# Two-block transformer kernel: the delta rule's decay steps a step later, the forgetting attention from long to short units, the last attention's scores in three pieces

## What is computed

```python
# forgetting attention: 16 heads of 64, query blocks of 128, causal
for i in range(S // BLK):
    lo, hi = i * BLK, (i + 1) * BLK
    s = einsum('bhqd,bhkd->bhqk', q[:, :, lo:hi], k[:, :, :hi]) * scale
    s = s + F[:, :, lo:hi, None] - F[:, :, None, :hi]
    p = softmax(where(causal, s, -inf), axis=-1)
    outs.append(einsum('bhqk,bhkd->bhqd', p, v[:, :, :hi]))

# delta rule, chunks of 128, 8 heads, once forward and once backward
decay = exp(where(tril, gc[..., :, None] - gc[..., None, :], -inf))
m = where(strict, einsum('bhncd,bhnsd->bhncs', kb, kc) * decay, 0.0)
tmat = triangular_solve(m + eye, eye, ...)          # the inverse
qk = einsum('bhncd,bhnsd->bhncs', qc, kc) * decay
def step(s, inp):
    v_new = u_i - w_i @ s
    o_i = qd_i @ s + qk_i @ v_new
    s = s * gl_i + kd_i.T @ v_new

# grouped-query attention: 8 heads of 64 on 2 key heads, 768 keys for each of 512 queries
o = softmax(q @ k.T * scale) @ v
```

## Time and profile before

| what | us |
| --- | --- |
| median of 3 runs (lowest, highest) | 3141.66 (3140.93, 3143.12) |
| the profiled execution | 3141.73 |
| its span in the profile | 3139.9 |
| PE busy in the span (22796 matmuls) | 2968.0 (95%) |
| DVE, ACT, POOL busy | 1669.5 (53%), 1214.1 (39%), 309.4 (10%) |
| forgetting attention, first score to last output | 661.04 to 758.18 |
| delta rule, steps 0 to 10 | 1337.03 to 1582.59 |
| GQA | about 2562 to 2638 |

### The profile page before, as it was taken

The page is one execution under the profiler, slowest core; times in us unless marked ns, Lnnn a source line. Parts: engine busy times, 40 slices in busy tenths (PEclk is TensorE's granted clock), DMA queues, the critical chain, the costliest instruction groups (busy, mean ns, idle before and its releaser), DMA issues.

```text
span 3139.9 us, 53876 instructions
## 1 busy us (share of the span) xinstructions
PE 2968.0 (95%) x22796; PEld 2420.2 (77%) x22796; DVE 1669.5 (53%) x2942; ACT 1214.1 (39%) x2193; POOL 309.4 (10%) x449
## 2 busy tenths in 40 slices
PE   7999999999999999978889999999999999999998
PEld 4767787766777688778766788888888877788887
DVE  3245666455533656677755553555556636554444
ACT  4315435356441455433345552111114437642221
POOL 1010020000001000043330010111110101000000
PEclk9999999989999999988889999999999999999999
DMA  6285542210314722001020022333342341032321
GB/s 230 81 296 183 187 156 89 94 55 18 106 69 173 264 101 71 22 18 29 24 69 28 1 74 81 124 120 119 121 146 76 93 75 48 8 107 101 107 94 67
DMA packets 180585, 308.11 MB, mean 98 GB/s; under 512 B 24038, under 2 KB 58151, under 8 KB 180089
## 3 DMA queue, kind: packets, MB, share of 16 engines
q1 hardware_dynamic: 141408, 253.87, 24.2%
q0 software_dynamic: 12048, 40.24, 4.2%
q10 hardware_dynamic: 26889, 10.56, 1.2%
HBM read 296.47 MB, written 6.81 MB: 97 GB/s over the span
## 4 chain that ended last, share of the span: by engine, by line
PE 78%; DVE 12%; ACT 6%; DMA 2%; issue 1%; POOL 0%; ACTq 0%; DVEq 0%; POOLq 0%
PE psum L428 20%; PE psum L429 20%; PE psum L430 20%; PE psum L1229 2%; DVE weights_r L370 2%; PE psum L2723 2%; PE psum L1257 1%; PE psum L1245 1%; DMA weights<-in_w_mod 1%; PE psum L621 1%; PE psum L2713 1%; DVE arena L917 1%; PE psum L1006 1%; PE psum L2825 1%; PE psum L1040 1%
## 5 line engine op out<-in xcount | busy, mean ns | idle before, releaser
L370 DVE TENSOR_TENSOR weights_r<-weights,weights_r 128x2048 fp32r<-128x2048 f32 (+1 forms) x161 | 360.5, 2259 | 379.9 <-ACT weights_r L361 379.9
L361 ACT ACTIVATE weights_r<-weights 128x2048 fp32r<-128x2048 f32 (+1 forms) x161 | 302.4, 1896 | 649.2 <-DMA weights<-in_w_ffn_gate 218.9
L428 PE MATMUL psum<-feat_r,weights_r 128*128 128x512 f32 (+1 forms) x1536 | 540.0, 352 | 1.2 <-ACT arena L2498 1.0
L429 PE MATMUL psum<-feat_r,weights_r 128*128 128x512 f32 (+1 forms) x1536 | 537.5, 350 | 0.0
L430 PE MATMUL psum<-feat_r,weights_r 128*128 128x512 f32 (+1 forms) x1536 | 536.7, 349 | 0.0
L428 PE MATMUL psum<-weights_r,feat_r 128*128 128x512 f32 (+2 forms) x1344 | 522.4, 389 | 12.1 <-DVE feat_r L762 8.8
L430 PE MATMUL psum<-weights_r,feat_r 128*128 128x512 f32 (+2 forms) x1344 | 517.4, 385 | 0.0
L429 PE MATMUL psum<-weights_r,feat_r 128*128 128x512 f32 (+2 forms) x1344 | 516.9, 385 | 0.0
L428 PEld LDWEIGHTS psum<-feat_r,weights_r 128*128 128x128 f32 x1536 | 294.4, 192 | 44.4 <-issue 5.4
L430 PEld LDWEIGHTS psum<-feat_r,weights_r 128*128 128x128 f32 x1536 | 293.9, 191 | 37.1
L429 PEld LDWEIGHTS psum<-feat_r,weights_r 128*128 128x128 f32 x1536 | 294.4, 192 | 36.3
(11 more groups left out here) (534 smaller groups left out, 4284.0 us busy)
## 6 DMA issues: line engine op xcount, KB each, us to landing
weights<-in_w_mod SPq DMA_DIRECT2D x30, 2048.0 KB, 16.6
weights<-in_gla_w_in SPq DMA_DIRECT2D x24, 1024.0 KB, 7.4
arena<-in_w_mod_turned POOLq DMA_DIRECT2D x96, 256.0 KB, 3.2
weights<-in_w_ffn_gate SPq DMA_DIRECT2D x22, 1024.0 KB, 6.9
weights<-in_w_ffn_up SPq DMA_DIRECT2D x22, 1024.0 KB, 5.1
weights<-in_w_ffn_down SPq DMA_DIRECT2D x20, 1024.0 KB, 6.9
weights<-in_fox_w_in SPq DMA_DIRECT2D x16, 1024.0 KB, 6.7
weights<-in_sgu_w_in SPq DMA_DIRECT2D x12, 1024.0 KB, 6.6
```

Source lines behind the costliest of these rows:

```text
L361: act.e.activation(WEI_r[:, s * SLOT + HALF:s * SLOT + HALF + n], WEI_t[:, s * SLOT:s * SLOT + n], ACT.Copy).then_inc(*A.put(("weights", c ...
L370: dve.e.tensor_tensor(WEI_r[:, s * SLOT:s * SLOT + n], WEI_t[:, s * SLOT:s * SLOT + n], WEI_r[:, s * SLOT + HALF:s * SLOT + HALF + n].bitc ...
L428: pe.e.matmul(ps, lh, rh, start=first, stop=False)
L429: pe.e.matmul(ps, lh, rl, start=False, stop=False)
```

## The change

Four edits. No instruction is added or taken away on DVE and POOL; ACT gets one more (the table load that stood ahead of the first exponential now belongs to it), and PE two more matmuls for each of GQA's 16 pairs.

- Delta rule, DVE: `dve_dif` and `dve_clamp` leave the end of step n-1 (where they worked for n+1) and stand in step n: the difference behind `dve_e(n,0)`, the clamp behind `dve_state(n)`. `dve_g(n,0)` stands ahead of `dve_state(n)`, and `dve_e(n,1)` ahead of `dve_kk(n+1)`.
- Delta rule, ACT: `act_decay_relu(n+1)` moves behind `act_cross(n-1)`, `act_decay_exp(n+1)` behind `act_et(n,1)`.
- Forgetting attention: the units run from t = 3 to t = 0, and ACT issues an exponential of one column (`act_exp_table`) ahead of its wait, so that the table is loaded there.
- GQA: the scores of a head are cut into three pieces of 256 columns, and the six pieces of a pair alternate between the two heads; the wait on itself stands before the fifth.

```diff
@@ pe_wide
-            for n, j in ((0, 0), (1, 0), (1, 1), (0, 1)):
+            count = len(units[2 * p]["scores"])
+            for n, j in ((0, 0), (1, 0), (1, 1), (0, 1)) if count < 3 else [(n, j) for j in range(count) for n in range(2)]:
                 unit = units[2 * p + n]
-                if j < len(unit["scores"]):
+                if j < count:
                     lt, rh, n0, w, first, end = unit["scores"][j]
                     c0 = n * unit["nk"] + n0
-                    if (n, j) == (0, 1):
+                    if (n, j) == (0, count - 1) and count > 1:
                         pe.wait_ge(*B.of((tag, "middle", p)))
                     done = pe.e.matmul(ps[:, c0:c0 + w], lt, rh, start=first, stop=end)
-                    if (n, j) == (1, 0) and len(unit["scores"]) > 1:
+                    if (n, j) == (1, 0) and count > 1:
                         done.then_inc(*B.put((tag, "middle", p)))
-                    if (n, j) == (1, 1):
+                    if (n, j) == (1, 1) and count == 2 or (n, j) == (0, 2):
                         done.then_inc(*B.put())
@@ fox_units
-        for t in LAT:
+        for t in LAT[::-1]:
@@ act_fox
         A.mark((T, "in"))
+        act_exp_table(act)
         act.wait_ge(*V.of((T, "in")))
@@ act_gdn
             if behind:
                 act_join_v(act, n - 1)
-            if more:
-                act_decay_relu(act, n + 1)
-                act_decay_exp(act, n + 1)
-            if behind:
                 act_join_z(act, n - 1)
                 act_cross(act, n - 1)
                 act_rows(act, n + 2)
+            if more:
+                act_decay_relu(act, n + 1)
             act_et(act, n, 1)
+            if more:
+                act_decay_exp(act, n + 1)
             if behind:
                 act_corner(act, n - 1)
@@ dve_gdn
             dve_e(dve, n, 0)
+            if more and behind:
+                dve_dif(dve, n + 1)
+            dve_g(dve, n, 0)
             dve_state(dve, n)
-            dve_g(dve, n, 0)
+            if more and behind:
+                dve_clamp(dve, n + 1)
             dve_x(dve, n, 0)
+            dve_e(dve, n, 1)
             if more:
                 dve_kk(dve, n + 1, 0)
                 dve_kk(dve, n + 1, 1)
-            dve_e(dve, n, 1)
             dve_g(dve, n, 1)
...
             dve_vb(dve, n)
-            if n + 2 < STEPS:
-                dve_dif(dve, n + 2)
-                dve_clamp(dve, n + 2)
@@ gqa_units
-                                          for n0, w in WIDE_CUTS[hh % 2]],
+                                          for n0, w in ((0, 256), (256, 256), (512, 256))],
```

## The result

The changed kernel takes 3218.61 us (median of four, 3212.28 to 3226.34), the kernel before 3142.39 beside it: a ratio of 1.024 (95% interval 1.021 to 1.026). It is slower, as forecast, but by 76 us and not by 15; the time lies outside the range of 3135 to 3168. The profiled execution took 3219.32 us with a span of 3217.5, so 77.6 more than the span of before, 3139.9.

A forecast was written before the change was run, and what follows sets the result against it. PE, holding 78% of the chain, was taken as the bound, running back to back outside the attentions and delta rule. 3141.7 + 21 (delta rule) - 2 (forgetting attention) - 4 (GQA) gave 3156 us, range 3135 to 3168.

The forecast's parts named there:

- Where the time goes: Delta rule: the 1.8 us idle ahead of `pe_e2(n,0)` goes; about 2.6 us comes ahead of `pe_kq(n,1)`, awaiting `dve_kk`.
- (1): Delta rule: the clock stays up despite the 2.6 us idle; 3135 us in all; chance 0.10.
- (2): At `pe_kq(n,1)`: PE does not wait for `dve_kk`, DVE alone sets 19.1 us steps; 3111 us; chance 0.08.
- (3): Delta rule: exponential starts earlier, `dve_kk` comes 1 us sooner, +8 there, 3143 to 3144 us in all; chance 0.12.
- The step at full clock: Delta rule: a step takes 21.4 us against 19.7, +1.7 each, +18.7 over steps 0 to 10.
- The low time: Delta rule: low clock stays 6.8 us a step, only later in the step; step 2 newly gets it, costing 2.7.
- 0.40 us per us: Delta rule: each us of low clock lengthens a step by 0.40 us, taken from the old steps' lengths.
- The upper bound: Delta rule: at most +30 us around about +21, with 5 more if all low time lies on PE's path.
- Step 11 and what follows: Delta rule's last step: nothing of the changed order's cost runs there, so the sum counts steps 0 to 10 only.
- Forgetting attention: Table load hidden -1.3, shorter last value products -1.5, longer first pair 0.5 to 0.8; sum -2 us.
- the rival inside the term: Forgetting attention's end: low clock reaches 3.4 to 6.8 us into the z layer, giving +1.4; no chance given.
- GQA: Scores of a pair take about 1.6 us against 1.86, -4 us over 16 pairs; with per-matmul overhead, 2.4 gained.

The follow-up runs named there:

- `gdn_alone`: The kernel before with only the delta rule's new order on VectorE and ScalarE; 3219.92 us (ratio 1.024).
- filled kernel: The changed kernel plus three extra 64x512 matmuls behind each corner product, in PE's idle ahead of the query-key products; 3168.08 us (ratio 1.007).
- `before_filled`: The kernel before plus four extra 128x256 matmuls ahead of join v in each step, in place of the 1.81 us idle; 3154.08 us (ratio 1.003).
- kernel with one extra matmul: The changed kernel plus one extra 64x512 matmul behind each corner product; 3177.26, 3206.46, 3216.55 and 3221.07 us in four executions.
- `three_parts`: The kernel before with first turn ahead of difference and clamp, clamp ahead of state product, GQA's three pieces and the early table load; 3133.62 us (ratio 0.997).

## Why the prediction was wrong, point by point

**Where the time goes: right.** The idle ahead of `pe_e2(n,0)` goes, one ahead of `pe_kq(n,1)` comes, ended by L3049 in each of steps 1 to 10, and it costs. (Its evidence was thinner than it says: two of the four waits of the earlier trace rows are weight loads'.) `gdn_alone` carries the whole loss. Rivals (1), (2) and (3) are all out: the clock does not stay up, PE does wait for `dve_kk`, and the exponential does not come sooner.

**The step at full clock: right, to a tenth.** The filled kernel lets it be read in its step 8 (zero 1532.92), beside step 6 of the changed kernel (zero 1501.42):

| point of the step, us | predicted | filled, full clock | changed, mostly 1.2 GHz |
|---|---|---|---|
| `pe_e2(n,0)` starts | 3.3 | 3.3 | 7.0 |
| clamp ends | 7.9 | 7.7 | 12.1 |
| `dve_x(n,0)` ends | 9.3 | 9.2 | 13.6 |
| `pe_corner` ends | 10.9 | 10.8 | 15.3 |
| `dve_kk` ends | 13.4 | 13.4 | 19.2 |
| step ends | 21.4 | 21.5 | 30.9 |

Steps of 21.41 and 21.51 without any low clock stand against the 21.4 of the sum. Step 2 as well: 19.28 + 1.7 + 2.7 = 23.7 forecast, 23.58 measured with 6.83 us low.

**The low time: this step failed.** The prediction said "I take the low time as the same, only later in the step", 6.8 us. It is 23.9 from step 5 on, and 203.2 instead of 78.5 in all. At the prediction's own 0.40 us per us that is 124.7 x 0.40 = 50 us, where the sum had 2.7. With this one term put right the sum gives 18.7 + 50 = 69 for steps 0 to 10; measured 65.8. The coefficient itself held: between the changed and the filled kernel, which have the same chain, it is (311.4 - 266.1) / 124.7 = 0.36.

What the runs show in its place looks like a loop. At 1.2 GHz (step 6 of the changed kernel against step 8 of the filled one) the state product takes 3.68 us instead of 2.00 and the products of the merge 1.82 instead of 1.04, so `dve_g` waits 3.40 us, the cross product is late, the relu that waits behind its copy holds up the copies of the second turn, and the idle ahead of the query-key products grows from 2.6 to 4.0. In steps 4 to 9 the clock is then down for 23.9 us, which covers all that makes the next idle long. The prediction had one half of this in a clause ("where the clock is low and `pe_cross` late, it holds these copies up as well") and gave it no price. That the wait brings the low clock is shown by filling it, which takes the low time back to 78.5. The added matmuls are also work, but work alone does not do it: two of them, 1.9 us, took 128 us off the low time here, and 2.0 us of them took 10 off in the old order (`before_filled`). That the two then keep each other up fits two more runs: shortening the wait by part gives a mixture of 24 us and 30 us steps, and one kernel with a wait in between takes 3177 us in one execution and 3221 in another.

Why the clock stays down for so long is not shown. The length of the wait does not set it alone. In the changed kernel's step 3 a wait of 3.90 us came with 3.41 us of low clock, in step 4 one of 3.18 with 23.89:

```profile
1434.48 2.08 PE L2715 MATMUL psum<-arena 64*128 64x128 f32 x16 [3.90 <-DVE weights L3049]
...
1459.08 2.08 PE L2715 MATMUL psum<-arena 64*128 64x128 f32 x16 [3.18 <-DVE weights L3049]
```

```profile
1434.47:1437.88 3.41, 3.40 (x69) 3.19 (x72) 0.24 (x2) 0.00 (x0) 2.94 (x6) 0.50 0.01 2
1458.36:1482.25 23.89, 23.17 (x448) 21.97 (x448) 12.72 (x30) 3.09 (x9) 7.58 (x14) 0.50 0.01 3
```

The Trainium skill (TensorE: Matmul & The Clock Gate, A second HAM failure mode: psum-queue depth-cycling) tells of a kernel whose clock goes up and down because PE stops shortly again and again while it cycles through PSUM banks. The trace agrees in that PE's waits for banks go with the falls: ten of them, 37.6 us. It differs in two things: these waits are of 2.8 to 4.0 us and one in a step, and where that kernel's median matmul stays at its full-clock value, here that of L2715 is 417 ns against 271.

**The upper bound** of +30 failed with it (its terms as they stand, 18.7 + 2.7 + 5, give 26). It asked what the known low time costs if it lies elsewhere, and not how long it can last. The earlier trace rows had a spell of 20.48 us with PE busy in 20.14 of them, as long as a step. Nearer still, the delta rule itself had one before the change, in step 3, which the earlier trace rows leave out. PE stood there for 4.26 us, from 1395.29 to 1399.55, the clock fell in this idle and stayed low for 20.48 us, and the step took 30.20 us:

```profile
1393.96:1424.16 30.20, 25.27 (x608) 23.51 (x608) 17.03 (x40) 7.81 (x15) 9.98 (x16) 0.66 0.07 20
1398.33:1418.81 20.48, 19.26 (x408) 17.95 (x408) 8.72 (x28) 6.94 (x13) 3.02 (x6) 0.50 0.10 29
```

```profile
1399.55 0.48 PE L2768 MATMUL psum<-feat,weights 32*32 32x32 f32 x4 [4.26 <-issue]
```

A bound of "every step low throughout", which step 10 of the kernel with one extra matmul shows as 31.5 us, would have been 11 x (31.5 - 22.3) = +101.

**Step 11 and what follows: not in the sum.** The spell that begins in step 10 lasts 30.7 us and reaches into step 11; 15.2 us more of low clock there, and 7.0 us. The other 6.1 us lie ahead of every changed line; kernels with the same code there reach that point anywhere from 646 to 653 us.

**Forgetting attention: the rival inside the term happened.** -2 forecast, +0.2 measured. The table load is out of the way, but the first scores are four times as long, so the first exponential starts 2.54 us behind them instead of 2.62: of the 1.28 nearly nothing is left. The tail is 0.6 shorter to the next layer's first matmul (96.26 us from the first scores instead of 96.89). And as the bounds had it, the spell of low clock has moved to the end and into that layer, by 2.25 us where the bounds had 3.4 to 6.8 (PEclk 0.50 to 765.46, the layer starts at 763.21):

```profile
748.39:765.46 17.07, 15.94 (x76) 9.76 (x77) 8.12 (x32) 11.64 (x41) 0.00 (x0) 0.50 0.01 1
```

```profile
763.21 0.78 PE L428 MATMUL psum<-weights_r,feat_r 128*128 128x512 f32 x1
763.79 0.63 PE L429 MATMUL psum<-weights_r,feat_r 128*128 128x512 f32 x1
...
766.18 0.39 PE L430 MATMUL psum<-weights_r,feat_r 128*128 128x512 f32 x1
```

**GQA: right.** Scores of 1.57 us against a forecast 1.6, 4.6 us in all against 4. The price per matmul that was weighed from the Trainium skill (TensorEngine Tiling (Array Packing), Instruction Overhead), by which an estimate of 2.4 was left, does not show: six pieces take less than 1.5 times the four of the neighbourhood attention (1.70).

## What to carry over

Where a step's length goes with the granted clock, price a new idle of PE by two cases, one at full clock and one in which the clock is low for the whole step, and ask whether the second lengthens the very idle that causes it: if it does, the low clock may last, as it did here from step 4 on. Count the wait of the decays, masks and other preparations by what stands behind them on the engine that frees the banks: a step of lookahead given up on an off-path engine came back here as 4 us on PE. And before a stall is explained by its wait, fill it: the filled kernel kept the whole chain of the wait, did more work, and was 50 us faster.

## What the hardware showed that was not expected

- TensorE stayed at 1.2 GHz for 23.9 us at a stretch while it was busy for 23.1 to 23.4 of them with small matmuls, in two different orders of work, and in `three_parts` for 27.31 us without any pause (the row below). Idles of about 1 us stand ahead of some falls, while steps with several of 0.6 to 0.9 us kept the full clock. What brings the clock back in these steps is not settled by these runs.
- One kernel's executions differ with this: the kernel before took 3131 to 3161 us over the study (its first three 3140.93 to 3143.12), and the kernel with one extra matmul 3177 to 3221. Over 70 executions of the kernel before, with the low time worked out from each one's mean clock (0.963 to 0.976), the time goes up by 0.31 us per us of low clock; one more, 3152.48 us at 0.921, does not fit.
- Without the long idle all kernels have 58 to 92 us of low clock in steps 0 to 10, whatever the order (132 and 133 where it was only shortened). What such a step would take with none of it is seen in single steps alone; at 0.40 us per us an estimate is 23 to 37 us less.

```profile
1534.70:1562.01 27.31, 27.31 (x566) 25.89 (x561) 15.97 (x40) 6.45 (x15) 8.87 (x15) 0.50 0.08 23
```
